# Four rows of the output stage loaded to one partition and repeated by TensorE instead of by the load

## The chip, the cores and the metric

The kernel runs on one core of one Trainium2 chip. The metric is the device time of one launch in microseconds (us): 4990.76 us, the median of three runs (4978.09 to 4993.18). The profiled execution took 4990.87 us, of which its trace spans 4988.1 us.

## The reference

One layer of a diffusion backbone runs over 128 context tokens and 512 latent tokens, of width 2048, in fp32: adaLN modulation, attention in two branches, an output projection with a gated residual, and then a PEER layer, in which each token picks 16 experts for each of 8 heads out of 16384 and gathers their rows. What the change touches is this part:

```python
    mod = jax.nn.silu(cond) @ p['w_ada'] + p['b_ada']
    sh1, sc1, g1, sh2, sc2, g2 = [m[:, None, :] for m in jnp.split(mod, 6, axis=-1)]
    ...
    x = x + g1 * (merged @ p['w_out'])

    h2 = rms_norm(x, p['norm2_g']) * (1 + sc2) + sh2
    x = x + g2 * peer_layer(h2, p['peer_w_query'], p['peer_sub_keys'], p['peer_u'], p['peer_v'])
```

The four rows of the title are g1, the gain norm2_g, the scale sc2 and the shift sh2. Each has 2048 numbers, one for each column and the same for all tokens of a group. With the tokens on the 128 partitions, an elementwise operation needs such a row in every partition.

## The kernel before

The 640 tokens are five blocks of 128, in three groups: group 0 is the context block, group 1 the first latent block, group 2 the other three latent blocks (`GROUP`, n = 1, 1, 3). For each group the kernel runs the branch products, the output stage, a norm, and the queries of the PEER layer. The three output stages lie at about 570 to 648 us, 1894 to 1959 us and 2564 to 2762 us of the span.

The output stage of a group has four chunks (`DCH` = 4) of 512 columns of `w_out`. The weights of a chunk come as two halves of 2 MB each, into a ring of three buffers (`WS` = 3), which SyncE fills in the order of use: a half is loaded as soon as TensorE has released the buffer of three halves before (`w_free`, L418). TensorE's `chunk` (L858) waits for a half, multiplies it with each of the n blocks (8 products of 128x128 by 128x512 for a half and a block, 16 for a chunk; the trace shows two matmul records for each such fp32 product), and releases it. In group 0 a panel of `w_ada` (2 MB, `ada`, L428 and L905) stands in the ring behind each chunk, so that group has three loads and three pieces of TensorE work to a chunk.

Around these loads SyncE issues, in its own order, the other transfers of the stage. Each of the four rows is read with `to_broadcast([P, D])`: 8 KB in DRAM, written 128 times, 1 MB into SBUF. Row g1 goes to `zone` when the transposes ahead of the stage are done (L623). In groups 0 and 1 the other three are issued after the second chunk's result was stored (`norm2_rows`, L617 to L619), ahead of the next halves. In group 2 sc2 and sh2 go out at L605 and L606, then g1 and the gain, all four ahead of the halves of the second chunk.

ScalarE copies each block's sums from PSUM to `zt` (`evac`, L1245), VectorE multiplies them by g1 and adds the residual (L1898 and L1900; in group 2 L1909 to L1913), and SyncE stores the result. Then VectorE forms (1 + sc2) * gain (L1547; in group 2 L1919), takes the norm, scales and shifts (L1557, L1558; in group 2 L1932, L1933), and TensorE turns the result for the queries (L886).

In group 2 the whole stage runs beside the PEER steps of group 1. For each token row GpSimd gathers 1 MB of expert rows (L766) into a ring of four buffers; VectorE takes a dot product with each (L1681, 16 of them), or adds each with a weight (L1691, 16), and only then frees the buffer. VectorE also chooses the experts of the next step in between (L1606 to L1660). Near its end this choice needs an exponential of ScalarE (`top_exps`, L1262): VectorE waits for `tk_exp` ahead of L1658. In ScalarE's order, the exponential of the first of these steps stands ahead of the evacuation of the stage's first block (`v in (0, 7)`).

PSUM has eight banks. The chunks use banks 0 to 1 or 0 to 3, the transposes banks 4 to 7, which are free while the output stage runs.

Of the kernel before, what the change touches and what calls it, by code (L numbers as in the profile page):

```python
# [8 lines left out]
D = 2048  # L9
# [67 lines left out]
U_OUT = tuple(u + 4 * DCH * g for u, g in zip(U_BR, GROUP))  # L77
U_QRY = tuple(u + DCH * g for u, g in zip(U_OUT, GROUP))

T_O = (NB, NB + 3, NB + 6)  # L80
T_M = tuple(t + g for t, g in zip(T_O, GROUP))
T_H = tuple(t + g for t, g in zip(T_M, GROUP))
EPS = 1e-6
SCALE = HD ** -0.5
LAM_INIT = 0.8 - 0.6 * math.exp(-0.3 * 0)
# [45 lines left out]
def build(nc, I, O):  # L131
# [34 lines left out]
    with ctx:  # L166
        def sb(name, shape, dt=f32):
            return ctx.enter_context(nc.sbuf_tensor(name, shape, dt))
# [8 lines left out]
        misc = sb("misc", [P, D])  # L177
        ident = sb("ident", [P, P])
        fold = sb("fold", [P, P])
        qts = sb("qts", [P, CH])  # L180
        small = sb("small", [P, 96])
        iota16 = sb("iota16", [P, TOPK])
# [14 lines left out]
        def zn(lo, n):  # L197
            return zone[:, lo:lo + n]
# [65 lines left out]
        def stay(c, lb):  # L264

            if c == DCH - 1:
                return zn(lb * CH, CH)
            places = [ac(A1 + 3 * D + CH * j, CH) for j in range(4)] + [zn(3 * CH, CH), zn(7 * CH, CH), zt[:, 3], zt[:, 4], qts[:, :]]
            return places[c * LAST + lb]

        def u_slot(i):

# [139 lines left out]
        def _(sp):  # L412
# [140 lines left out]
            for g in range(3):  # L553
# [46 lines left out]
                if g == 2:  # L600
                    sp.wait_ge(mm_done, U_OUT[2])
                    for lb in range(n):
                        sp.dma_start(xb[lb], xs[block_of(g, lb)]).then_inc(G["xt"][lb], 16)
                    sp.wait_ge(t_done, 4 * (T_M[g] + n))
                    sp.dma_start(A, mod[cnd:cnd + 1, 4 * D:5 * D].to_broadcast([P, D])).then_inc(s["row"], 16)  # L605
                    sp.dma_start(Bv, mod[cnd:cnd + 1, 3 * D:4 * D].to_broadcast([P, D])).then_inc(s["row"], 16)  # L606
                if g == 1:
                    sp.wait_ge(mm_done, U_OUT[1])
                    sp.dma_start(ac(A1, D), final_row).then_inc(fa_in, 16)
# [4 lines left out]

                def norm2_rows():

                    sp.dma_start(gain, I["norm2_g"].to_broadcast([P, D])).then_inc(s["row"], 16)  # L617
                    sp.dma_start(A, mod[cnd:cnd + 1, 4 * D:5 * D].to_broadcast([P, D])).then_inc(s["row"], 16)
                    sp.dma_start(Bv, mod[cnd:cnd + 1, 3 * D:4 * D].to_broadcast([P, D])).then_inc(s["row"], 16)  # L619

                if g == 0:
                    ada_rows(6)
                sp.dma_start(zn(0, D), mod[cnd:cnd + 1, 2 * D:3 * D].to_broadcast([P, D])).then_inc(G["g1"], 16)  # L623
                if g < 2:
                    sp.dma_start(zn(D, D), xs[0] if g else xp[0]).then_inc(G["xt"][0], 16)
                else:
                    sp.dma_start(gain, I["norm2_g"].to_broadcast([P, D])).then_inc(s["row"], 16)
                for c in range(DCH):
                    if g == 0:
                        ada(A_OUT + c)  # L630
# [91 lines left out]
        def _(pool):  # L722
# [9 lines left out]
            for n, v in enumerate(("lambda_q1", "lambda_k1", "lambda_q2", "lambda_k2")):  # L732
# [5 lines left out]
            nc.gpsimd.iota(iota16[:, :], pattern=[[1, TOPK]], base=0, channel_multiplier=0,  # L738
                           allow_small_or_imprecise_dtypes=True).then_inc(mats, 1)

            nc.gpsimd.memset(fold[:, :], 0.0).then_inc(mats, 1)
            for d in range(-3, 4):
                pool.wait_ge(mats, d + 7)
# [103 lines left out]
        def _(pe):  # L847
# [10 lines left out]
            def chunk(acts, n, i, step, blocks, u, bank_of, depth):  # L858

                for h in range(2):  # L860
                    wait_half(n + h, i, step)
                    for b in range(blocks):
                        if h == 0:
                            pe.wait_ge(bank_free, u + b + 1 + NB - depth)
                        ins = products(acts[:, h * (KT // 2):(h + 1) * (KT // 2)], b, n + h, bank_of(b), h == 0, h == 1)
                        if h == 1:
                            ins.then_inc(mm_done, 1)
                    if h == 0:
                        ins.then_inc(w_free, 1)
                release(u + blocks)  # L870

            def release(u):

# [174 lines left out]
            for g in range(3):  # L1048
# [55 lines left out]
                for lb in range(n if g == 2 else 0):  # L1104
                    for q in range(4):
                        pe.wait_ge(G["br"], B * DCH + q * n + lb + 1)
                        quarter(T_M[g] + lb, q, stay(q, lb))
                pe.wait_ge(t_free, (T_M[g] + n) * 4 + 4)
                for c in range(DCH):
                    chunk(mT[g], H_OUT[g] + 2 * c if g else RING_AT["out", 2 * c], 0, 0, n, U_OUT[g] + c * n, lambda b: bk(c * n + b), DEPTH[g])  # L1110
                    if g == 0:
                        ada(A_OUT + c)

# [127 lines left out]
        def _(sa):  # L1241
# [133 lines left out]
            for g in range(3):  # L1375
# [124 lines left out]
        def _(dve):  # L1500
# [39 lines left out]
            def norm(s, g, b, T0):  # L1540
# [2 lines left out]
                R, x = s["again"], xb[b % 2]  # L1543
                assert g != 2
                if b == 0 or (b == 1 and g == 3):
                    dve.wait_ge(s["row"], 48 * (1 + R) if b == 0 else 80)
# [326 lines left out]
            for g in range(3):  # L1873
# [28 lines left out]
                def residual_2(v):  # L1902

                    c, lb = v // n, v % n
                    x1 = nbuf[2][0][lb][:, c * CH:(c + 1) * CH]
                    if v == 0:
                        dve.wait_ge(G["g1"], 16 * (1 + B))
                    dve.wait_ge(bank_free, U_OUT[2] + v + NB + 1)
                    link(V.tensor_tensor(zt[:, v % 4], zt[:, v % 4], zn(c * CH, CH), ALU.mult))  # L1909
                    if c == 0:  # L1910
                        dve.wait_ge(G["xt"][lb], 16)
                    link(V.tensor_tensor(x1, x1, zt[:, v % 4], ALU.add))
                    signal(V.tensor_tensor_reduce(out=zt[:, v % 4], in0=x1, in1=x1, scale=1.0, scalar=0.0, op0=ALU.mult, op1=ALU.add,  # L1913
                                                  accum_out=small[:, 40 + 4 * lb + c:41 + 4 * lb + c]), G["ou"], B * DCH + v + 1)

                def scale_row():

                    dve.wait_ge(nrm[2]["row"], 48)
                    link(V.scalar_tensor_tensor(nbuf[2][2], nbuf[2][2], 1.0, nbuf[2][4], ALU.add, ALU.mult))  # L1919

                def norm_2(lb):
# [23 lines left out]
                        peer_step(1, PH + c, c % 2, PH + c)  # L1945
                        merge(c)
                if g < 2:
                    dve.wait_ge(G["g1"], 16 * (1 + B))
# [163 lines left out]
```

## Time and profile before

| | us |
|---|---|
| median of three runs | 4990.76 |
| lowest, highest | 4978.09, 4993.18 |
| the profiled execution | 4990.87 |
| its span in the trace | 4988.1 |
| PE busy | 3316.5 (66%) |
| DVE busy | 2717.3 (54%) |
| POOL busy | 1853.9 (37%) |
| ACT busy | 452.8 (9%) |

The page gives the whole span first: how busy each engine is, and in 40 slices of 125 us each engine, TensorE's granted clock (in tenths) and the DMA engines. The three output stages lie in slices 5 to 6, 16 and 21 to 23 of the 40:

```profile
PE   4869989899698898999999861333333333333334
DVE  2330128988134202577778888656565656565653
PEclk7989999999799999999999985555555555555555
DMA  9978988899899678999999999999999999999998
```

A digit of 9 means 90% and more. In these slices both TensorE and the DMA engines are near full, so neither line alone tells which one a stage waits for. For that one has to go to the stage itself: to TensorE's own instructions in order of time, with what ended each idle time before them.

### The profile page before, as it was taken

The numbers are of one execution on the slowest core, as the hardware profiler recorded it, in microseconds if no ns is written. First come the engines' busy times: TensorE is split into PE (matmuls) and PEld (weight loads), VectorE is DVE, ScalarE is ACT, GpSimd is POOL, SyncE is SP. The second block draws the span as 40 slices with busy tenths as digits, with TensorE's granted clock in tenths as the row PEclk, the third lists the DMA queues.
The fourth block names the chain that finished last, engine by engine and source line by source line (L and its number), as shares of the span: only waits on it lengthen the run. The fifth ranks groups of instructions, "written<-read, shape, count | busy, mean of one in ns | idle before, by whom it ended". The sixth has DMA issues, their size and how long they took to land.

```text
span 4988.1 us, 32667 instructions
## 1 busy us (share of the span) xinstructions
PE 3316.5 (66%) x11402; PEld 1292.2 (26%) x11402; DVE 2717.3 (54%) x4132; ACT 452.8 (9%) x824; POOL 1853.9 (37%) x1365
## 2 busy tenths in 40 slices
PE   4869989899698898999999861333333333333334
PEld 0333333344244443444444430000000000000000
DVE  2330128988134202577778888656565656565653
ACT  0010010000122201111110110000000000000000
POOL 0000004444233000244434565564545555555542
PEclk7989999999799999999999985555555555555555
DMA  9978988899899678999999999999999999999998
GB/s 380 385 292 326 357 303 313 324 357 368 348 391 404 250 283 301 357 365 366 370 389 396 379 410 373 421 421 421 421 411 418 421 421 421 415 416 421 421 421 336
DMA packets 407517, 1869.35 MB, mean 375 GB/s; under 512 B 30016, under 2 KB 33632, under 8 KB 238160
## 3 DMA queue, kind: packets, MB, share of 16 engines
q0 software_dynamic: 187200, 1347.98, 66.1%
q1 hardware_dynamic: 220176, 519.60, 28.0%
q8 instruction: 75, 1.23, 0.1%
q14 instruction: 66, 0.54, 0.0%
HBM read 1835.65 MB, written 33.13 MB: 375 GB/s over the span
## 4 chain that ended last, share of the span: by engine, by line
DMA 47%; PE 33%; DVE 11%; issue 5%; POOL 2%; ACT 1%; SPq 0%; DVEq 0%; POOLq 0%; ACTq 0%; PEldq 0%
PE ps L854 24%; DMA activations<-in_peer_v,zt 19%; DMA big<-in_peer_v,zt 15%; DMA big<-in_w_in 3%; DMA big<-in_peer_u,sel 3%; DVE big L1744 2%; DMA big<-in_peer_v,zone 2%; PE ps L1232 2%; DMA big<-in_peer_w_query 2%; DMA big<-in_w_ada 2%; PE ps L954 2%; PE ps L1014 2%; DVE big L1691 1%; PE ps L992 1%; PE ps L905 1%
## 5 line engine op out<-in xcount | busy, mean ns | idle before, releaser
L854 PE MATMUL ps<-big,activations 128*128 128x512 f32 x4096 | 1806.6, 601 | 89.6 <-ACT zt L1245 27.4
L854 PEld LDWEIGHTS ps<-big,activations 128*128 128x128 f32 x4096 | 782.0, 193 | 1097.5 <-issue 1006.4
L2066 DVE CUSTOM_DVE_ANT_0 big<-big,activations 128x2048 f32<-128x2048 f32 x256 | 585.2, 2291 | 492.2 <-DMA big<-in_peer_u,sel 492.1
L836 POOL DMA_INDIRECT big<-in_peer_u,sel x384 | 505.8, 1317 | 594.8 <-DVE zt L2066 501.6
L1232 PE MATMUL ps<-activations,zt 128*32 128x512 f32 x1536 | 333.8, 959 | 506.8 <-DMA activations<-in_peer_v,zt 506.8
L1232 PE MATMUL ps<-big,zt 128*32 128x512 f32 x1536 | 350.8, 1033 | 471.7 <-DMA big<-in_peer_v,zt 369.3
L2066 DVE CUSTOM_DVE_ANT_0 big<-big,zone 128x2048 f32<-128x2048 f32 x128 | 291.4, 2291 | 212.3 <-DMA big<-in_peer_u,sel 212.1
L842 POOL DMA_INDIRECT big<-in_peer_v,zt x192 | 306.2, 1595 | 155.8 <-PE ps L1232 126.2
L805 POOL DMA_INDIRECT big<-in_peer_u,sel x128 | 213.2, 1666 | 292.9 <-DVE zone L1744 258.4
L1744 DVE CUSTOM_DVE_ANT_0 big<-big 128x2048 f32<-128x2048 f32 x128 | 289.1, 2290 | 42.3 <-DMA big<-in_peer_u,sel 41.0
L1691 DVE SCALAR_TENSOR_TENSOR big<-big,work 128x2048 f32<-128x2048 f32 x115 | 270.5, 2352 | 62.2 <-DMA big<-in_peer_v,sel 58.7
L1681 DVE CUSTOM_DVE_ANT_0 big<-big 128x2048 f32<-128x2048 f32 x114 | 259.8, 2289 | 68.7 <-DMA big<-in_peer_u,sel 67.7
L842 POOL DMA_INDIRECT activations<-in_peer_v,zt x192 | 216.2, 1126 | 177.9 <-PE ps L1232 128.8
L749 POOL DMA_DIRECT2D mod_rows<-work x12 | 6.2, 520 | 662.9 <-DVE work L1535 662.9
L854 PE MATMUL ps<-big 128*128 128x512 f32 x544 | 242.3, 604 | 11.9 <-DMA big<-in_w_in 10.3
L766 POOL DMA_INDIRECT big<-in_peer_v,sel x96 | 169.6, 1767 | 196.2 <-DVE big L1691 148.4
L1232 PEld LDWEIGHTS ps<-activations,zt 128*32 128x32 f32 x1536 | 40.0, 136 | 780.3 <-DMA activations<-in_peer_v,zt 738.6
L1232 PEld LDWEIGHTS ps<-big,zt 128*32 128x32 f32 x1536 | 47.1, 148 | 735.7 <-DMA big<-in_peer_v,zt 553.4
L766 POOL DMA_INDIRECT big<-in_peer_u,sel x96 | 153.4, 1598 | 224.0 <-DVE work L1681 181.6
L1195 PE MATMUL ps<-small,zt 128*128 128x16 f32 x48 | 14.3, 378 | 329.4 <-DVE zt L1865 329.4
L811 POOL DMA_INDIRECT big<-in_peer_v,zone x128 | 122.0, 953 | 270.1 <-PE ps L954 211.2
L1785 DVE TENSOR_REDUCE small<-ps 128x1 f32<-128x640 f32 (+1 forms) x80 | 57.4, 718 | 259.7 <-PE ps L992 259.0
(215 smaller groups left out, 2734.4 us busy)
## 6 DMA issues: line engine op xcount, KB each, us to landing
big<-in_w_in SPq DMA_DIRECT2D x84, 2048.0 KB, 10.2
big<-in_w_ada SPq DMA_DIRECT2D x48, 2048.0 KB, 12.4
big<-in_w_out SPq DMA_DIRECT2D x24, 2048.0 KB, 14.6
big<-in_peer_w_query SPq DMA_DIRECT2D x24, 2048.0 KB, 9.6
big<-in_w_branch_a SPq DMA_DIRECT2D x12, 2048.0 KB, 12.6
big<-in_w_branch_b SPq DMA_DIRECT2D x12, 2048.0 KB, 9.7
big<-z_blocks SPq DMA_DIRECT2D x20, 512.0 KB, 13.1
big<-in_peer_u,sel POOLq DMA_INDIRECT x626, 10.6
```

Of the source, the lines that this page charges most:

```text
L766: pool.indirect_dma_start(slot(j), None, eu if j < TOPK else ev, bass.IndirectOffsetOnAxis(ap=sel[:, q, j % TOPK:j % TOPK + 1], axis=0)).t ...
L805: pool.indirect_dma_start(slot(m), None, eu, bass.IndirectOffsetOnAxis(ap=sel[:, t % 2, k:k + 1], axis=0)).then_inc(ring_in[m % RING], 16)
L811: pool.indirect_dma_start(v_slot_0(n), None, ev, bass.IndirectOffsetOnAxis(ap=idx_t0[:, n:n + 1], axis=0)).then_inc(v_in[n % VR_0], 16)
L836: pool.indirect_dma_start(u_slot(m), None, eu, bass.IndirectOffsetOnAxis(ap=sel[:, t % 2, k:k + 1], axis=0)).then_inc(u_in[m % UR], 16)
L842: pool.indirect_dma_start(v_slot(m), None, ev, bass.IndirectOffsetOnAxis(ap=idx_v[(t - 1) % 3][:, k:k + 1], axis=0)).then_inc(v_in[m % VR] ...
L854: ins = nc.tensor.matmul(bank(bk), acts[:, k, b * P:(b + 1) * P], w[:, n % WS, k], start=(start and k == 0), stop=(stop and k == KT // 2 - 1))
L954: ins = nc.tensor.matmul(ps[32 * j:32 * j + 32, 7 * 512:8 * 512], spread_0[q % 2][:, i * 32:(i + 1) * 32], v_slot_0(n)[:, j * CH:(j + 1) * ...
L1232: ins = nc.tensor.matmul(ps[32 * j:32 * j + 32, q * 512:(q + 1) * 512], spread[(t - 1) % 2][:, k * 32:(k + 1) * 32], v_slot(m)[:, j * CH:( ...
L1681: V.tensor_tensor_reduce(out=t, in0=t, in1=hcur, scale=1.0, scalar=0.0, op0=ALU.mult, op1=ALU.add, accum_out=dots[:, k:k + 1]).then_inc(ri ...
L1691: signal(V.scalar_tensor_tensor(acc, tile(TOPK + k), coef[:, k:k + 1], acc, ALU.mult, ALU.add), ring_free, m * 32 + RING + TOPK + k + 1)
L1744: V.tensor_tensor_reduce(out=slot(m), in0=slot(m), in1=hcur, scale=1.0, scalar=0.0, op0=ALU.mult, op1=ALU.add, accum_out=dots_0[:, m:m + 1 ...
L2066: V.tensor_tensor_reduce(out=x, in0=x, in1=h_of[ph], scale=1.0, scalar=0.0, op0=ALU.mult, op1=ALU.add, accum_out=dots_s[t % 2][:, k:k + 1] ...
```

## The change

The rows are loaded as they are, 8 KB to one partition. A tile `ones` (1 x 128) is filled once by GpSimd. For each row TensorE forms four products, `ones` (1 x 128) by 512 numbers of the row (1 x 512), into banks 4 to 7, and ScalarE copies the four banks over the row's tile, all 128 partitions. The products stand between and within the chunks (`ROW_AT` gives chunk and half for each row), the copies ahead of certain evacuations (`ROW_OUT`). VectorE waits for the copies in place of the loads. The counters of the transposes (`T_O`, `T_M`, `T_H`) are moved by the four rows.

```diff
-T_O = (NB, NB + 3, NB + 6)
+ROWS = 4
+T_O = (NB, NB + 3 + ROWS, NB + 6 + 2 * ROWS)
 T_M = tuple(t + g for t, g in zip(T_O, GROUP))
-T_H = tuple(t + g for t, g in zip(T_M, GROUP))
+T_R = tuple(t + g for t, g in zip(T_M, GROUP))
+T_H = tuple(t + ROWS for t in T_R)
...
+        def row_of(g, i):
+
+            return (zn(0, D), nbuf[g][2], nbuf[g][3], nbuf[g][4])[i]
+
+        ROW_AT = ({(0, 1): 0, (2, 0): 1, (2, 1): 2, (3, 0): 3},) * 2 + ({(0, 0): 0, (1, 0): 1, (1, 1): 2, (2, 0): 3},)
+        ROW_OUT = ({1: (0,), 2: (1,), 3: (2, 3)},) * 2 + ({0: (0,), 3: (1,), 6: (2, 3)},)
...
                 def norm2_rows():
 
-                    sp.dma_start(gain, I["norm2_g"].to_broadcast([P, D])).then_inc(s["row"], 16)
-                    sp.dma_start(A, mod[cnd:cnd + 1, 4 * D:5 * D].to_broadcast([P, D])).then_inc(s["row"], 16)
-                    sp.dma_start(Bv, mod[cnd:cnd + 1, 3 * D:4 * D].to_broadcast([P, D])).then_inc(s["row"], 16)
+                    sp.dma_start(gain[0:1], I["norm2_g"]).then_inc(s["row"], 16)
+                    sp.dma_start(A[0:1], mod[cnd:cnd + 1, 4 * D:5 * D]).then_inc(s["row"], 16)
+                    sp.dma_start(Bv[0:1], mod[cnd:cnd + 1, 3 * D:4 * D]).then_inc(s["row"], 16)
 
                 if g == 0:
                     ada_rows(6)
-                sp.dma_start(zn(0, D), mod[cnd:cnd + 1, 2 * D:3 * D].to_broadcast([P, D])).then_inc(G["g1"], 16)
+                sp.dma_start(zn(0, D)[0:1], mod[cnd:cnd + 1, 2 * D:3 * D]).then_inc(G["g1"], 16)
...
+            nc.gpsimd.memset(ones[:, :], 1.0)
...
                     if h == 0:
                         ins.then_inc(w_free, 1)
+                        behind(0)
                 release(u + blocks)
+                behind(1)
...
+                def row_turn(c, h):
+
+                    if (c, h) not in ROW_AT[g]:
+                        return
+                    i = ROW_AT[g][c, h]
+                    if i == 0:
+                        pe.wait_ge(G["g1"], 16 * (1 + B))
+                    if i == 1:
+                        pe.wait_ge(nrm[g]["row"], 48 * (1 + R))
+                    for q in range(4):
+                        pe.wait_ge(t_free, (T_R[g] + i) * 4 + q + 1)
+                        nc.tensor.matmul(bank(4 + q), ones[:, :], row_of(g, i)[0:1, q * CH:(q + 1) * CH],
+                                         start=True, stop=True).then_inc(t_done, 1)
...
+                def row_out(i):
+
+                    for q in range(4):
+                        sa.wait_ge(t_done, (T_R[g] + i) * 4 + q + 1)
+                        nc.scalar.activation(row_of(g, i)[:, q * CH:(q + 1) * CH], bank(4 + q), ACT.Copy).then_inc(t_free, 1)
+
                 for c in range(DCH):
                     for lb in range(n):
                         v = c * n + lb
+                        for i in ROW_OUT[g].get(v, ()):
+                            row_out(i)
                         if v == 0:
                             sa.wait_ge(G["zt"], 2 * DCH * (n + R) + ZTS[g])
```

The loads of group 2 (L605, L606, L623, L627) are changed in the same way. In VectorE's program the waits for the loads ahead of L1547, L1898, L1909 and L1919 become waits for `t_free`.

## Rows read from the trace of the kernel before

**Rows 1.** The page: the shares of the chain that ended last, by engine.
```profile
DMA 47%; PE 33%; DVE 11%; issue 5%; POOL 2%; ACT 1%; SPq 0%; DVEq 0%; POOLq 0%; ACTq 0%; PEldq 0%
```

**Rows 2.** Timeline of PE, output stage of group 0: start, duration, instruction, idle before.
```profile
569.82 14.00 PE L854 MATMUL ps<-big,activations 128*128 128x512 f32 x32 [1.06 <-ACT activations L1251]
583.97 1.90 PE L905 MATMUL ps<-big,small 128*2 128x512 f32 x16
588.48 15.70 PE L854 MATMUL ps<-big,activations 128*128 128x512 f32 x32 [2.61 <-DMA big<-in_w_out]
...
606.15 14.00 PE L854 MATMUL ps<-big,activations 128*128 128x512 f32 x32
625.52 3.59 PE L905 MATMUL ps<-big,small 128*2 128x512 f32 x16 [5.37 <-DMA big<-in_w_ada]
630.94 16.93 PE L854 MATMUL ps<-big,activations 128*128 128x512 f32 x32 [1.83 <-DMA big<-in_w_out]
```

**Rows 3.** Windows, group 0: stretch, engines' busy us, then clock, DMA share, GB/s.
```profile
588.00:604.00 16.00, 15.53 (x32) 6.61 (x32) 0.00 (x0) 0.00 (x0) 0.00 (x0) 0.89 0.94 356
...
613.00:631.00 18.00, 10.81 (x34) 3.32 (x32) 3.12 (x4) 0.60 (x1) 0.00 (x0) 0.78 1.02 404
```

**Rows 4.** Timeline of SyncE's queue in the same stage.
```profile
606.87 0.39 SPq L617 DMA_DIRECT2D big<-in_norm_g  x1
...
608.25 0.43 SPq L428 DMA_DIRECT2D big<-in_w_ada  x1
```

**Rows 5.** The 12 DMAs of bias rows (tile in_b_ada), 8 KB each: time to landing.
```profile
DMA to landing us min/median/max: 1.8/4.9/5.8
```

**Rows 6.** DMA issues between 613 and 625 us: count, size, us to landing.
```profile
x_blocks<-zt SPq DMA_DIRECT2D x1, 256.0 KB, 15.9
```

**Rows 7.** Timeline of PE, output stage of group 1.
```profile
1894.01 14.00 PE L854 MATMUL ps<-big,activations 128*128 128x512 f32 x32 [1.06 <-ACT activations L1251]
...
1922.75 13.97 PE L854 MATMUL ps<-big,activations 128*128 128x512 f32 x32 [0.46 <-PE ps L854]
1943.30 16.11 PE L854 MATMUL ps<-big,activations 128*128 128x512 f32 x32 [6.58 <-DMA big<-in_w_out]
```

**Rows 8.** Timeline of SyncE's queue in the same stage.
```profile
1925.56 0.45 SPq L617 DMA_DIRECT2D big<-in_norm_g  x1
...
1928.17 5.72 SPq L419 DMA_DIRECT2D big<-in_w_out  x2
```

**Rows 9.** Timeline of ACT, output stage of group 2.
```profile
2575.89 1.28 ACT L1262 ACT_TABLE_LOAD   x1 [12.36 <-DVE work L1630]
2577.18 0.31 ACT L1262 ACTIVATE work<-work 128x16 f32<-128x16 f32 x1
...
2591.36 0.60 ACT L1245 ACTIVATE zt<-ps 128x512 f32<-128x512 f32 x1 [13.77 <-PE ps L854]
```

**Rows 10.** Timeline of DVE in the same stage.
```profile
2583.51 0.16 DVE L1658 RECIPROCAL work<-work 128x1 f32<-128x1 f32 x1
...
2594.35 2.29 DVE L1681 CUSTOM_DVE_ANT_0 big<-big 128x2048 f32<-128x2048 f32 x1 [0.94 <-DMA big<-in_peer_u,sel]
...
2762.30 0.69 DVE L1909 TENSOR_TENSOR zt<-zt,zone 128x512 f32<-128x512 f32 x1
```

**Rows 11.** Waits of DVE between 2556 and 2614 us: total, times, longest.
```profile
DVE big L1681 <- DMA big<-in_peer_u,sel: 9.0, 9, 1.7
```

**Rows 12.** Timeline of PE, first and last chunk of group 2 (three blocks each).
```profile
2563.59 41.47 PE L854 MATMUL ps<-big,activations 128*128 128x512 f32 x96 [1.24 <-ACT activations L1251]
...
2696.91 41.47 PE L854 MATMUL ps<-big,activations 128*128 128x512 f32 x96 [3.45 <-DMA big<-in_w_out]
```

**Rows 13.** DMA queues between 2587 and 2600 us: packets, MB, share of 16 engines.
```profile
q0 software_dynamic: 576, 4.19, 77.9%
q1 hardware_dynamic: 576, 1.18, 24.2%
```

**Rows 14.** The gathers issued between 720 and 800 us: time to landing.
```profile
DMA to landing us min/median/max: 7.1/9.3/12.9
```

More of the change, by code:

```diff
@@ L179, in build @@
         fold = sb("fold", [P, P])
+        ones = sb("ones", [1, P])
         qts = sb("qts", [P, CH])
@@ L615, in norm2_rows @@
                 def norm2_rows():
-                    sp.dma_start(gain, I["norm2_g"].to_broadcast([P, D])).then_inc(s["row"], 16)
-                    sp.dma_start(A, mod[cnd:cnd + 1, 4 * D:5 * D].to_broadcast([P, D])).then_inc(s["row"], 16)
-                    sp.dma_start(Bv, mod[cnd:cnd + 1, 3 * D:4 * D].to_broadcast([P, D])).then_inc(s["row"], 16)
+                    sp.dma_start(gain[0:1], I["norm2_g"]).then_inc(s["row"], 16)
+                    sp.dma_start(A[0:1], mod[cnd:cnd + 1, 4 * D:5 * D]).then_inc(s["row"], 16)
+                    sp.dma_start(Bv[0:1], mod[cnd:cnd + 1, 3 * D:4 * D]).then_inc(s["row"], 16)
                 if g == 0:
                     ada_rows(6)
-                sp.dma_start(zn(0, D), mod[cnd:cnd + 1, 2 * D:3 * D].to_broadcast([P, D])).then_inc(G["g1"], 16)
+                sp.dma_start(zn(0, D)[0:1], mod[cnd:cnd + 1, 2 * D:3 * D]).then_inc(G["g1"], 16)
                 if g < 2:
@@ L626, in _ @@
                 else:
-                    sp.dma_start(gain, I["norm2_g"].to_broadcast([P, D])).then_inc(s["row"], 16)
+                    sp.dma_start(gain[0:1], I["norm2_g"]).then_inc(s["row"], 16)
                 for c in range(DCH):
@@ L856, in products, with chunk @@
                 return ins
-            def chunk(acts, n, i, step, blocks, u, bank_of, depth):
+            def chunk(acts, n, i, step, blocks, u, bank_of, depth, behind=lambda h: None):
                 for h in range(2):
@@ L1108, in _ @@
                 pe.wait_ge(t_free, (T_M[g] + n) * 4 + 4)
+                def row_turn(c, h):
[10 more added lines that the diff above has]
+                                         start=True, stop=True).then_inc(t_done, 1)
                 for c in range(DCH):
-                    chunk(mT[g], H_OUT[g] + 2 * c if g else RING_AT["out", 2 * c], 0, 0, n, U_OUT[g] + c * n, lambda b: bk(c * n + b), DEPTH[g])
+                    chunk(mT[g], H_OUT[g] + 2 * c if g else RING_AT["out", 2 * c], 0, 0, n, U_OUT[g] + c * n, lambda b: bk(c * n + b), DEPTH[g], lambda h: row_turn(c, h))
                     if g == 0:
@@ L1545, in norm @@
                 if b == 0 or (b == 1 and g == 3):
-                    dve.wait_ge(s["row"], 48 * (1 + R) if b == 0 else 80)
+                    if g == 3:
+                        dve.wait_ge(s["row"], 48 if b == 0 else 80)
+                    else:
+                        dve.wait_ge(t_free, (T_R[g] + ROWS) * 4 + 4)
                     link(V.scalar_tensor_tensor(A, A, 1.0, gain, ALU.add, ALU.mult))
@@ L1906, in residual_2 @@
                     if v == 0:
-                        dve.wait_ge(G["g1"], 16 * (1 + B))
+                        dve.wait_ge(t_free, (T_R[2] + 1) * 4 + 4)
                     dve.wait_ge(bank_free, U_OUT[2] + v + NB + 1)
@@ L1916, in scale_row @@
                 def scale_row():
-                    dve.wait_ge(nrm[2]["row"], 48)
+                    dve.wait_ge(t_free, (T_R[2] + ROWS) * 4 + 4)
                     link(V.scalar_tensor_tensor(nbuf[2][2], nbuf[2][2], 1.0, nbuf[2][4], ALU.add, ALU.mult))
@@ L1947, in _ @@
                 if g < 2:
-                    dve.wait_ge(G["g1"], 16 * (1 + B))
+                    dve.wait_ge(t_free, (T_R[g] + 1) * 4 + 4)
                     for v in range(DCH * n):
```

## The prediction

> **What bounds the kernel now.** I read four views, in this order. First the page's chain that ended last: it is 47% DMA and 33% PE [rows 1], so both a transfer taken away and TensorE work added can move the end; which of them does, only the stage tells. Second, TensorE's timeline of each output stage, for its idle times and what ended them. In group 0 TensorE waits 2.61 us for a half of w_out, 5.37 us for a panel of w_ada and 1.83 us for the next half [rows 2]. Third, the windows around two of these waits: granted clock 0.89 and 0.78, DMA share 0.94 and 1.02 [rows 3]. So part of each stretch ran at the lower of the two levels, 1.2 instead of 2.4 GHz, and the durations agree: the same 32 records took 14.00 us in two chunks, 15.70 and 16.93 us in the two behind a wait, the same 16 of w_ada 1.90 and 3.59 us [rows 2]. This stage is bound by its loads and pays for it in idle time and in clock. In group 1 one wait is left, 6.58 us ahead of the last chunk, which then took 16.11 us [rows 7]; the rest of that stage is TensorE at full clock. Fourth, VectorE's waits in group 2, where the gathers set the pace: 9.0 us in nine waits between 2556 and 2614 [rows 11].
>
> **The loads removed.** Twelve rows of 1 MB become 8 KB each. At the 404 GB/s of the stretch at 613 [rows 3] one is 1.05 MB / 404 = 2.6 us of all DMA engines. Three are issued at 606.87, ahead of the w_ada panel at 608.25 [rows 4], which comes 5.37 us late; their 7.8 us cover this wait and the 1.83 behind it. The fourth, g1, lies ahead of the half that is 2.61 us late, and is worth as much. I let all three waits go.
>
> **The products added.** This is the term that decides. A chunk is 16 products (two halves of 8) and shows as 32 records in 14.00 us [rows 2], so a product of 512 columns is 14.00 / 16 = 0.88 us, not 0.44. A row of the change is four products: 3.5 us, four rows 14.0 us. The trace has no product over a single partition, so I bound it by its neighbours. High end: the chunk at a mixed clock, 16.93 / 16 = 1.06 us, 17 us for four rows. Low end: the panel of w_ada, 8 products of 512 columns in 1.90 us, 0.24 us each [rows 2], 3.8 us for four rows; but these have two output rows each and write four parts of a bank, while the new ones have 128 outputs, as those of a chunk. I take 0.88.
>
> One page bears on the low end. The Trainium skill, TensorE: Matmul & The Clock Gate, section Why this matters for your kernels, says that a single product over 32 rows takes as long as one over 128. By it a row costs 3.5 us, as taken; no row of this trace shows a product over so few rows.
>
> **Group 0.** Now the stage runs from 569.82 to 630.94 + 16.93 = 647.87, 78.05 us [rows 2]. Afterwards: four chunks 4 x 14.00 = 56.0, three panels 3 x 1.90 = 5.7, the rows 14.0, and 0.3 between chunks, 0.9: 76.6. Gain 1.4 us. What is late next? A half is issued when its buffer comes free and needed two pieces of work later, at the least a half and a panel, 8.9 us, and mostly a row more; with fewer bytes ahead of it that suffices. The new wait is TensorE's for the three small loads ahead of row 1. Behind it on TensorE queue the second half of the third chunk and all that follows. By this sum chunk 1 ends at about 603.7, its store goes out at about 606, the loads are issued by 607.7, and row 1 stands at 612.9. Loads of 8 KB landed in 1.8 to 5.8 us, median 4.9 [rows 5]: no wait. With the high price of a product the group loses 1.6; with the loads late it loses more (below). ScalarE's copies, 16 of 0.60 us [rows 9] in a group, cost nothing in groups 0 and 1: ScalarE waits for the chunks there. The last ones lie in the last half-chunk, 7 us, so VectorE's chain behind the stage finds its rows ready. If that cover were gone, 2.4 us a row.
>
> **Group 1.** Now 1894.01 to 1943.30 + 16.11 = 1959.41, 65.4 us [rows 7]. Afterwards 56.0 + 14.0 + 0.9 = 70.9: a loss of 5.5 us, though the wait of 6.58 us and the low clock behind it (16.11 - 14.00 = 2.1) are gone; 8.7 us of gain pay for 14.0 us of products. The loads ahead of the last half, from 1925.56 to 1928.17 [rows 8], are those that made it late. Row 1 comes due at about 1933.1, and the small loads are issued by about 1930, behind 1 MB of output (2.6 us): landing at the median would make TensorE wait 1.4 us more. Loss 6.9, between 4.3 (no wait, and a gap or two less) and 10.
>
> **Group 2.** TensorE has room here: its last block is done at 2696.91 + 41.47 = 2738.4 [rows 12] and taken by VectorE at 2762.30 [rows 10], so 14 us of rows hide in 23.9. Two other things count. First a gain: of VectorE's waits, 9.0 us [rows 11] come from gathers that share the DMA engines with the loads. With the queues both full, each gets as many packets, 576 and 576, but 4.19 MB for the gathers against 1.18 MB [rows 13], since a gather's packets are longer; so 4 MB less ahead of the weights' two halves empties that queue early, and the gathers have the engines to themselves. They would then land in some 7.1 to 9.3 us [rows 14] after issue, and with four buffers and a dot product of 2.29 us [rows 10] part of each wait stays. Second a cost, hidden in ScalarE's order: row 0's copies stand ahead of the exponential. The row's products come after the first half of the chunk, 2563.59 + 41.47 / 2 = 2584.3 [rows 12], end at 2587.8, the last copy at 2588.5; then the table load and the exponential, 1.28 + 0.31 and some 0.2 [rows 9]: 2590.3. VectorE needs it at 2583.51 [rows 10]. Behind this wait are queued all its dot products, so it stands 6.8 us. The four buffers fill meanwhile: the next four dots run without the 0.94 us [rows 10] of before them, and the others wait less. Following them one by one with a landing of 8 us, the sixteenth ends at about 2616.9, against 2616.7: gain and stall cancel. I take 0; the ends are -6.8 (nothing returned) and +9 (all waits gone and the stall hidden).
>
> **The sum** against the profiled execution, 4990.87 us, which is 0.1 from the median: +1.4 - 6.9 + 0 = -5.5, so 4996.4. All behind the stages follows by dependence, and I let the shifts pass to the end.
>
> **Rivals.**
> 1. Products over one partition are short (0.24 us). Group 0: 56 + 5.7 + 3.8 + 0.9 = 66.4, of which the loads, that need their 8 us each, may let 9 us be gained; group 1 gains 65.4 - 60.7 = 4.7, less 1; group 2 perhaps 2. 4976. Against it: the number of outputs is that of a full product.
> 2. Group 2 pays: the freed queue gives back the 9.0 us and the stall hides. 4988. For it, DMA is full there; against it, VectorE's stall is plain in ScalarE's order.
> 3. The stall of group 2 stays whole and products cost the high price: 4996.4 + 6.8 + 2 x 3 = 5009. It decides where gathers land later than about 9 us after issue.
> 4. The small loads are late. A store of 256 KB issued in this stage took 15.9 us to land [rows 6], since the queue ahead of it was full. At 15.9 row 1 of group 0 would come at 623.5 instead of 612.9, that of group 1 at 1946 instead of 1933: 10.6 and 11.4 more, 5018. From about 6 us of landing group 0 starts to lose, group 1 from about 3.
> 5. The change doesn't do what it says: the weights' waits come from the ring of three buffers and not from the rows. Then the rows' 14 us add to 78 in group 0, part of them inside the waits. With 8 us lost there: 5006.
>
> One page speaks against the change where rival 4 does. The Trainium skill, DMA: Bandwidth & Descriptors, section Bandwidth, says that transfers under 64 KB are dominated by their descriptors, and wants 1 MB at least. By it the small loads waste the engines; the bias rows, 4.9 us [rows 5], show only their latency.
>
> **How the numbers follow.** The forecast has 0.56, rival 1 0.10, rival 2 0.12, rival 3 0.10, rival 4 0.06, rival 5 0.06. The range leaves out the outer part of rivals 1, 4 and 5: 4983 to 5010. About 0.3%, 15 us, is what a measurement here can tell from no change; so faster (below 4975.9) has only part of rival 1 and a tail, 0.09; slower (above 5005.7) has rivals 3, 4 and part of 5, 0.18; the same 0.73.
>
> **What would show it.** Right: in group 0 no wait of TensorE for w_ada; each row's four products last 3.5 us; group 1's stage 70 to 73 us; VectorE idle for 6 to 7 us ahead of the L1658 that now stands at 2583.51, released by ScalarE. Wrong: rows of products under 2 us or over 5; a wait of TensorE of over 3 us ahead of row 1; halves still late in group 0; VectorE's end of group 2's stage moved by over 5 us.

## The result: slower by 0.64%, outside the range

| | us |
|---|---|
| kernel before, median of 5 runs | 4990.76 (4978.09 to 4994.51) |
| changed kernel, median of 5 runs | 5020.47 (5013.49 to 5030.88) |
| ratio, 95% interval | 1.0064 (1.0050 to 1.0077) |
| forecast, range | 4996.4 (4983 to 5010) |
| profiled execution of the changed kernel | 5030.88, its span 5029.2 |

The profiled execution is the slowest of the five, so the traces lie 41.1 us apart (5029.2 - 4988.1) where the medians lie 29.7 apart. A second profiled execution of the same kernel is among the experiments. The page of the changed kernel, its busy times and the chain:

```profile
PE 3379.6 (67%) x11498; PEld 1315.2 (26%) x11498; DVE 2716.2 (54%) x4132; ACT 481.8 (10%) x872; POOL 1864.2 (37%) x1366
...
DMA 44%; PE 37%; DVE 11%; issue 4%; POOL 2%; ACT 1%; SPq 0%; another core or an unknown queue 0%; DVEq 0%; POOLq 0%; ACTq 0%; PEldq 0%
```

Four points of the chain went over to TensorE, 37% for 33%, and DMA has 44% for 47% [rows 1]. TensorE is busy 63.1 us longer. The products, at 3.67 us a row (below), make 12 x 3.67 = 44 of that; what the other 19 are, only the stages tell. TensorE's timeline of group 1's output stage (start, duration, instruction, idle before):

```profile
1907.42 14.00 PE L865 MATMUL ps<-big,activations 128*128 128x512 f32 x32 [1.06 <-ACT activations L1278]
1921.72 5.16 PE L1133 MATMUL ps<-zone,ones 1*128 1x512 f32 x8 [0.30 <-PE ps L865]
1926.81 15.85 PE L865 MATMUL ps<-big,activations 128*128 128x512 f32 x32
1942.97 7.10 PE L865 MATMUL ps<-big,activations 128*128 128x512 f32 x16 [0.30 <-PE ps L865]
1951.31 4.10 PE L1133 MATMUL ps<-activations,ones 1*128 1x512 f32 x8 [1.23 <-DMA activations<-mod_rows]
1955.34 10.08 PE L865 MATMUL ps<-big,activations 128*128 128x512 f32 x16
1965.57 4.64 PE L1133 MATMUL ps<-activations,ones 1*128 1x512 f32 x8
1970.14 9.51 PE L865 MATMUL ps<-big,activations 128*128 128x512 f32 x16
...
1984.56 9.13 PE L865 MATMUL ps<-big,activations 128*128 128x512 f32 x16
```

The wait for w_out of 6.58 us [rows 7] is gone, and the longest wait left is 1.23 us, for the small loads. Yet the stage takes 86.3 us, from 1907.42 to 1993.69, where it took 65.4. No work is missing its data; the same work is slower. A half-chunk behind a row takes 9.13 to 10.08 us where half of a 14.00 us chunk is due, and the rows take 4.10 to 5.16. The windows over both stages (busy us of PE, PEld, DVE, ACT, POOL, then granted clock, DMA share, GB/s) say why:

```profile
570.00:656.10 86.10, 84.54 (x208) 32.58 (x208) 9.02 (x10) 11.36 (x20) 0.52 (x1) 0.90 0.81 291
1907.40:1993.70 86.30, 84.28 (x160) 33.75 (x160) 13.70 (x13) 12.81 (x21) 0.00 (x0) 0.84 0.66 234
```

TensorE is busy for 84.28 of 86.30 us, and its granted clock is 0.84: part of a stage with hardly any idle time ran at 1.2 instead of 2.4 GHz. The kernel before had 0.95 in this stage. In group 0 it was 0.89 before, with TensorE idle for 10.2 of 78.1 us; now it is 0.90 with 1.6 of 86.1 idle, so there the idle time went and the low clock stayed. Behind rows 0 and 1:

```profile
590.27 15.12 PE L865 MATMUL ps<-big,activations 128*128 128x512 f32 x32
607.36 7.13 PE L865 MATMUL ps<-big,activations 128*128 128x512 f32 x16
615.06 3.69 PE L1133 MATMUL ps<-activations,ones 1*128 1x512 f32 x8 [0.57 <-DMA activations<-mod_rows]
618.69 8.83 PE L865 MATMUL ps<-big,activations 128*128 128x512 f32 x16
```

Where the clock is full, a row is 3.67 us and a half 7.13. Along the span the 41.1 us come in as +0.2 ahead of group 0's stage, +8.0 in it (78.05 to 86.0), +5.2 between the two stages, +20.9 in group 1's, -0.1 up to group 2, +8.0 in group 2, and -1.0 in the rest. The 5.2 us lie in code that is unchanged: that stretch took 1246.1 us in the profiled execution of the kernel before, and 1247.2 to 1256.7 in the eleven of this and the later kernels, 1252.9 in the one that has neither products nor small loads. Scatter of single executions, with the one of before at its low end, would explain it; with one profile of the kernel before it is not shown.

### The profile page after: what moved, and what is told of

Read it like the earlier page. It is cut to its first block, busy times and chain, and to the rows that moved or that the text cites. A ratio compares the mean times of both kernels' runs of the same rounds, so it can differ in the third digit from the quotient of the medians.

```text
span 5029.2 us, 32914 instructions
## 1 busy us (share of the span) xinstructions
PE 3379.6 (67%) x11498; PEld 1315.2 (26%) x11498; DVE 2716.2 (54%) x4132; ACT 481.8 (10%) x872; POOL 1864.2 (37%) x1366
## 3 DMA queue, kind: packets, MB, share of 16 engines
q0 software_dynamic: 187200, 1347.98, 65.7%
## 4 chain that ended last, share of the span: by engine, by line
DMA 44%; PE 37%; DVE 11%; issue 4%; POOL 2%; ACT 1%; SPq 0%; another core or an unknown queue 0%; DVEq 0%; POOLq 0%; ACTq 0%; PEldq 0%
PE ps L865 27%; DMA activations<-in_peer_v,zt 17%; DMA big<-in_peer_v,zt 16%; DMA big<-in_w_in 3%; DVE big L1782 2%; PE ps L1259 2%; DMA big<-in_w_ada 2%; PE ps L967 2%; PE ps L1027 2%; DMA big<-in_peer_u,sel 2%; DMA big<-in_peer_v,zone 2%; PE ps L1005 1%; DVE big L1729 1%; PE ps L918 1%; DMA big<-in_peer_w_query 1%
## 5 line engine op out<-in xcount | busy, mean ns | idle before, releaser
L847 POOL DMA_INDIRECT big<-in_peer_u,sel x384 | 509.4, 1327 | 593.1 <-DVE zt L2104 499.6
L816 POOL DMA_INDIRECT big<-in_peer_u,sel x128 | 216.2, 1689 | 286.3 <-DVE zone L1782 250.9
L777 POOL DMA_INDIRECT big<-in_peer_u,sel x96 | 159.3, 1660 | 221.3 <-DVE work L1719 176.7
```

Of the source, the lines that this page charges most:

```text
L777: pool.indirect_dma_start(slot(j), None, eu if j < TOPK else ev, bass.IndirectOffsetOnAxis(ap=sel[:, q, j % TOPK:j % TOPK + 1], axis=0)).t ...
L816: pool.indirect_dma_start(slot(m), None, eu, bass.IndirectOffsetOnAxis(ap=sel[:, t % 2, k:k + 1], axis=0)).then_inc(ring_in[m % RING], 16)
L847: pool.indirect_dma_start(u_slot(m), None, eu, bass.IndirectOffsetOnAxis(ap=sel[:, t % 2, k:k + 1], axis=0)).then_inc(u_in[m % UR], 16)
```

## The experiments

Theory: products over a single partition, though they follow each other without idle time, leave TensorE's granted clock to fall, and all work of the stage pays for that. The rivals: TensorE is slow because it waits (for small loads or weights); the loads were never what the stage waited for; the cost lies in group 2's order of ScalarE. Stages are told by length, from the start of the first chunk to the end of the last.

### The same products over all 128 partitions

```diff
-        ones = sb("ones", [1, P])
+        ones = sb("ones", [P, P])
...
-            nc.gpsimd.memset(ones[:, :], 1.0)
+            nc.gpsimd.memset(ones[:, :], 0.0).then_inc(ones_ok, 1)
+            pool.wait_ge(ones_ok, 1)
+            nc.gpsimd.memset(ones[0:1, :], 1.0).then_inc(ones_ok, 1)
...
-                        nc.tensor.matmul(bank(4 + q), ones[:, :], row_of(g, i)[0:1, q * CH:(q + 1) * CH],
+                        nc.tensor.matmul(bank(4 + q), ones[:, :], row_of(g, i)[:, q * CH:(q + 1) * CH],
```

> The changed kernel with one edit: the stationary operand of the row products is 128x128 (first row ones, the rest zeros) and the moving one takes all 128 partitions of the row's tile, so each product is a full one with the same outputs. Theory (the granted clock falls because a product over one partition leaves TensorE nearly idle): granted clock 1.00 in the stages of groups 0 and 1, the pieces behind a row again 7.1 and 14.0 us, stage of group 0 at 77 to 79 us instead of 86.1, of group 1 at 71 to 73 instead of 86.3, and the whole 15 to 25 us below the changed kernel's 5020 (ratio to before 1.001 to 1.004). Rival (the clock falls because of the short gaps or waits around the rows, or from TensorE's total load): both stages stay at 85 to 87 us and the ratio at 1.006.

Measured: 5000.87 us, median of 12, against 4990.76; ratio 1.0019 (1.0011 to 1.0028). Timeline of PE in group 1, and the windows over groups 0 and 1:

```profile
1895.38 14.00 PE L868 MATMUL ps<-big,activations 128*128 128x512 f32 x32 [1.06 <-ACT activations L1281]
1909.68 3.67 PE L1136 MATMUL ps<-zone,ones 128*128 128x512 f32 x8 [0.30 <-PE ps L868]
1913.19 13.90 PE L868 MATMUL ps<-big,activations 128*128 128x512 f32 x32
...
1935.73 3.70 PE L1136 MATMUL ps<-activations,ones 128*128 128x512 f32 x8 [1.20 <-DMA activations<-mod_rows]
1939.26 7.03 PE L868 MATMUL ps<-big,activations 128*128 128x512 f32 x16
```
```profile
567.70:645.00 77.30, 75.90 (x208) 30.76 (x208) 9.03 (x10) 11.35 (x20) 0.52 (x1) 1.00 0.90 326
1895.40:1967.30 71.90, 69.89 (x160) 29.96 (x160) 13.71 (x13) 12.77 (x21) 0.00 (x0) 1.00 0.78 280
```

Same number of products, same order, same loads, and a wait of 1.20 us for them at the same place; only the rows that take part differ. The clock is 1.00, the halves behind a row take 7.03 us, and the stages 77.3 and 71.9 us instead of 86.0 and 86.3. That is the theory, and it accounts for 8.7 + 14.4 = 23.1 us of the profiled executions; the medians lie 19.6 apart (5020.47 - 5000.87). The result of a product is the same in both, since 127 of its rows meet a zero. The edit widens both operands of the product, so which of the two the clock answers to is not told apart.

### The products added to the kernel before, its loads kept

```diff
+                    for q in range(4):
+                        nc.tensor.matmul(bank(4 + q), ident[0:1, :], misc[0:1, q * CH:(q + 1) * CH], start=True, stop=True)
```

They stand at the change's places, and nobody reads them. A second kernel takes `ident[:, :]` and `misc[:, ...]`, all 128 partitions.

> The kernel before, all its loads as they are, with 4 x 4 products over one partition added in each stage at the places of the change; nothing reads them, nothing waits for them. Theory: the clock falls in group 1's stage: 65.4 + 14.7 + some 9 of clock, less the wait of 6.6 for the late half that is covered: 80 to 84 us; group 0's stage 84 to 90. Rival (the copies, the waits for them or the small loads lower the clock): group 1's stage 72 to 75 us at clock 1.00. Ratio to before by the theory 1.003 to 1.006, by the rival 1.001 to 1.003.

> The same as e2_before_plus_one_row but with the products over all 128 partitions. Theory: 3.5 to 3.7 us a row and the clock of the stages at 1.00 except behind waits for loads: group 1's stage 72 to 74 us, some 8 to 10 less than with one partition. Rival: the same as with one partition, within 2 us.

Measured: 5010.34 us (ratio 1.0033, 1.0020 to 1.0046) over one partition, 5001.12 (1.0012, 1.0003 to 1.0021) over all. Group 1, two lines of the one, then two of the other, then the window of each:

```profile
1927.04 3.70 PE L1118 MATMUL ps<-misc,ident 1*128 1x512 f32 x8
1930.66 15.62 PE L854 MATMUL ps<-big,activations 128*128 128x512 f32 x32
```
```profile
1915.82 3.67 PE L1118 MATMUL ps<-misc,ident 128*128 128x512 f32 x8
1919.33 13.90 PE L854 MATMUL ps<-big,activations 128*128 128x512 f32 x32
```
```profile
1912.90:1989.30 76.40, 75.80 (x160) 31.24 (x160) 13.70 (x13) 3.23 (x5) 0.00 (x0) 0.93 0.87 319
```
```profile
1901.70:1971.90 70.20, 69.60 (x160) 30.04 (x160) 13.71 (x13) 3.22 (x5) 0.00 (x0) 1.00 0.93 346
```

The pair repeats the difference without the change's loads, copies and waits: clock 0.93 against 1.00, stage 76.5 against 70.3. The sign is as expected, both sizes were missed: I had expected 80 to 84 and 72 to 74 us. With one-partition products the changed kernel loses 14.4 us here, this one 6.2. In group 0 the stage took 88.7 us at a clock of 0.87 with no wait of TensorE above 0.33 us, as expected (84 to 90), and 82.2 at 0.96 over all partitions, where a wait of 3.06 us for w_out stands. There the clock is lower than in the changed kernel (0.90). So how far the clock falls is not given by the products alone.

### The small loads alone

The changed kernel without the products and copies; the tiles' other 127 rows stay as they were. What is left out is in the expectation.

> The changed kernel with only its small loads: no products of the rows and no copies, so 127 partitions keep old numbers in the four rows' tiles (the rows are missing there; the output and the experts that are chosen follow from that, the amount of work does not). It gives the gain of the loads alone. My sum: group 0's three waits go, stage 62 to 64 us instead of 78.05; group 1's wait goes, stage 57 to 58 instead of 65.4; VectorE's waits in group 2 between its first dot products fall from 9.0 to under 6 us. Whole: ratio 0.993 to 0.996. Rival (the waits for weights come from the ring of three buffers): group 0 at 72 us or more.

Measured: 4967.51 us, ratio 0.9947 (0.9934 to 0.9960), stages 64.3 and 56.8 us. Group 1 is the bare work, 4 x 14.00 and the gaps, and all its waits are gone. So the weights' waits did come from the 1 MB loads, and taking them away is worth 8.6 us in group 1 and 13.8 in group 0. The stages had been expected at 62 to 64 and 57 to 58, so both sizes were nearly met. In group 2 the expectation for the gathers, waits under 6 us, fails. VectorE's waits for them, over the same 58 us of the stage as rows 11:

```profile
DVE big L1717 <- DMA big<-in_peer_u,sel: 8.6, 7, 2.3
```

8.6 us where the kernel before has 9.0. Over this stretch the kernels without a stall and with small loads (this one and three below) have 6.9 to 8.6 us, those with the 1 MB loads 8.7 to 10.3. Four megabytes less ahead of the weights give the gathers little.

### The exponential ahead of row 0's copies

The kernel with the products over 128 partitions, and in group 2:

```diff
+                        if g == 2 and v == 0:
+                            top_exps(PH + 5)
                         for i in ROW_OUT[g].get(v, ()):
                             row_out(i)
```

(the second call stays ahead of the evacuation of v == 7)

> e1_full_rows with ScalarE's first exponential of group 2's stage put ahead of row 0's copies. Theory A of the prediction (the stall of 6.9 us and the gathers' gain cancel): the stall goes, and from the first product of the stage to the first product behind it (L1225's first, 396.1 us in e1_full_rows) 2 to 5 us are gained; ratio 0.0005 to 0.001 lower than e1_full_rows. Theory B (the gathers have nothing to give, the stall costs in full): 7 us gained. Theory C (the DMA engines set the pace there): no gain.

Measured: 4999.92 us, ratio 1.0021 (1.0012 to 1.0030), so in the whole nothing that can be told from 1.0019. I had expected 0.0005 to 0.001 less. VectorE's waits in group 2 over the 58 us of rows 11, of the changed kernel, of the one with full rows, and of this one (engine, line, releaser: total, times, longest):

```profile
DVE work L1696 <- ACT work L1289: 7.1, 1, 7.1
...
DVE big L1719 <- DMA big<-in_peer_u,sel: 3.1, 4, 1.6
```
```profile
DVE work L1699 <- ACT work L1292: 6.9, 1, 6.9
...
DVE big L1722 <- DMA big<-in_peer_u,sel: 2.8, 5, 1.1
```
```profile
DVE big L1724 <- DMA big<-in_peer_u,sel: 6.9, 7, 2.7
```

The stall of 6.9 us goes; the waits for gathers rise from 2.8 to 6.9, and the group is 3.2 us shorter (392.9 against 396.1, one execution each). Of the stall, 4.1 us had been paid back by buffers that filled during it.

### The kernel before with three loads later

```diff
-                    if g < 2 and c == 1:
+                    if g < 2 and c == 2:
```

in SyncE's program, at the condition that guards `norm2_rows()`: in groups 0 and 1 the three 1 MB loads go out behind the last weights of the stage. Not one byte is saved, and there are no products. In group 1 the same condition also guards a store of 1 MB of finished output. It moves along: before, it stood ahead of the last half of w_out, now behind it.

```profile
1924.91 0.59 SPq L648 DMA_DIRECT2D out<-activations  x1
```
```profile
1939.94 0.37 SPq L648 DMA_DIRECT2D out<-activations  x1
```

> The kernel before with one edit: in groups 0 and 1 SyncE issues its three 1 MB row loads behind the store of the third chunk instead of the second, so behind the halves of the last chunk. If these loads did harm only because they stood ahead of weights: group 0's stage 66 to 70 us instead of 78.05, group 1's 57 to 59 instead of 65.4, and nothing is given back by the norm behind the stage; ratio 0.995 to 0.997. Rival (the bytes count, wherever they stand): the norm waits for its rows or the queries' weights come late, and the ratio is 0.999 to 1.000.

Measured: 4975.74 us, ratio 0.9971 (0.9962 to 0.9980), stages 67.8 and 56.9 us, 0.1 from the bare work in group 1. What the loads and the store are worth apart in group 1 is not told by this run; in the kernel with the small loads alone the store stayed where it was and no wait was left. This is the best version of the study that computes everything. The wait for w_ada did not go away, it stands behind the stage:

```profile
627.92 14.00 PE L854 MATMUL ps<-big,activations 128*128 128x512 f32 x32 [1.82 <-DMA big<-in_w_out]
647.69 3.59 PE L905 MATMUL ps<-big,small 128*2 128x512 f32 x16 [5.77 <-DMA big<-in_w_ada]
```

There TensorE's panel is not what comes next for the norm, and the 5.77 us lie beside VectorE's work: from the end of the stage to the first product that waits for the norm it is 12.2 us, as before.

### The changed kernel once more

No edit.

> The changed kernel once more, unedited, beside the others of this call and with a second profile. Its stages should again be 8 and 15 to 21 us longer than before's, at a granted clock of 0.84 to 0.93 in group 1's; the 5.2 us that the first profile lost between the two stages, where nothing was changed, should not come back if they were the scatter of one execution, and should if the change did them. Ratio 1.005 to 1.0075.

Measured: 5030.67 us, median of 6, ratio 1.0078 (1.0062 to 1.0094), stages 85.4 and 84.6 us. The clock's fall is no accident of one execution; it was 0.92 and 0.86 in the two stages. Group 2 came out at +5.0 us instead of +8.0. The stretch between the first two stages, which was to lose its 5.2 us if they were scatter, came at 1254.4 us, 8.3 above the kernel before.

### Four products side by side

Here each small load writes partitions 0, 32, 64 and 96, and product q takes partition 32 q, to see whether the four of a row then run at once; the exponential stands first.

```diff
-                    sp.dma_start(gain[0:1], I["norm2_g"]).then_inc(s["row"], 16)
+                    sp.dma_start(gain[0:97:32], I["norm2_g"].to_broadcast([4, D])).then_inc(s["row"], 16)
...
-                        nc.tensor.matmul(bank(4 + q), ones[:, :], row_of(g, i)[0:1, q * CH:(q + 1) * CH],
+                        nc.tensor.matmul(bank(4 + q), ones[32 * q:32 * q + 1, :], row_of(g, i)[32 * q:32 * q + 1, q * CH:(q + 1) * CH],
```

> The changed kernel with each row loaded to the partitions 0, 32, 64 and 96 (32 KB), and its four products taken from one of these each, so that they can run side by side in the array; the exponential stands first as in e5_full_rows_exp_first. If they run side by side a row takes 0.9 to 1.0 us instead of 3.7 and the clock stays: group 0's stage 66 to 69 us, group 1's 61 to 63, ratio 0.996 to 0.998. If they run one after the other, as in the changed kernel: 3.7 us a row, falling clock, ratio 1.005. If side by side but the clock falls all the same: stages 3 to 8 us longer than the first figures.

Measured: 4988.31 us, median of 12, ratio 0.9999 (0.9989 to 1.0009), stages 72.7 and 67.8 us. The row's time is as expected, the stages (66 to 69 and 61 to 63) and the ratio (0.996 to 0.998) were missed. Group 1:

```profile
1910.78 1.14 PE L1133 MATMUL ps<-zone,ones 1*128 1x512 f32 x8 [0.30 <-PE ps L865]
1911.85 14.00 PE L865 MATMUL ps<-big,activations 128*128 128x512 f32 x32
...
1936.19 1.69 PE L1133 MATMUL ps<-activations,ones 1*128 1x512 f32 x8 [2.94 <-DMA activations<-mod_rows]
1937.82 9.93 PE L865 MATMUL ps<-big,activations 128*128 128x512 f32 x16
```

A row is 1.14 us instead of 3.67, still over single partitions, and the chunk behind it takes 14.00 us, the full clock; the halves behind rows 2 and 3 take 7.13 each. Only behind the wait of 2.94 us for the small loads does the clock fall, and in group 0 behind one of 1.78 us. So no row of 1.14 us is followed by slow work where no wait stood; but row 1 now comes due earlier, and the loads are late for it. The Trainium skill, TensorE: Matmul & The Clock Gate, section Part 3: Packing small matmuls — row/col tiling, gives 3.07 times for four products over 32 rows each, placed so. The trace, with one row each, agrees: 3.67 / 1.14 = 3.2.

### The small loads one chunk earlier

Two kernels with `if g < 2 and c == 0:` as the condition that guards `norm2_rows()`, one made from the changed kernel, one from that with four products side by side. In group 1 the 1 MB store of finished output moves ahead with the small loads here too.

> The changed kernel with the three small loads of groups 0 and 1 issued behind the store of the first chunk instead of the second, so that TensorE doesn't wait for them ahead of row 1. Theory (the clock falls by the one-partition products themselves): group 1's stage loses the 1.2 us of waiting and little more: 80 to 85 us at a clock of 0.84 to 0.92, ratio 1.005 to 1.007. Rival (in the changed kernel it is this wait that lets the clock fall, and so the 8 to 10 us between its group 1, 86.3, and that of e2_before_plus_one_row, 76.5): 75 to 77 us, ratio 1.003.

> e8_four_row_groups with the small loads issued a chunk earlier, in the same way. There the waits for them, 1.78 and 2.94 us, were each followed by a half of 10.0 instead of 7.1 us. If the wait is what let the clock fall there: group 0's stage 67 to 69 us instead of 72.7, group 1's 61 to 63 instead of 67.8, ratio 0.997 to 0.999. If the short rows do it: the halves behind row 1 stay at 9 to 10 us.

Measured: the first 5019.34 us, ratio 1.0058 (1.0045 to 1.0071), stages 83.7 and 80.0; the second 4983.01 us, ratio 0.9988 (0.9979 to 0.9997), stages 73.8 and 65.2. Group 1 of the first, with its window, then of the second:

```profile
1915.84 3.99 PE L1133 MATMUL ps<-zone,ones 1*128 1x512 f32 x8 [0.30 <-PE ps L865]
1919.76 17.03 PE L865 MATMUL ps<-big,activations 128*128 128x512 f32 x32
...
1944.12 5.01 PE L1133 MATMUL ps<-activations,ones 1*128 1x512 f32 x8
1949.06 9.16 PE L865 MATMUL ps<-big,activations 128*128 128x512 f32 x16
```
```profile
1901.50:1981.50 80.00, 79.20 (x160) 32.19 (x160) 13.70 (x13) 12.83 (x21) 0.00 (x0) 0.89 0.71 252
```
```profile
1925.69 8.83 PE L865 MATMUL ps<-big,activations 128*128 128x512 f32 x16 [2.38 <-DMA big<-in_w_out]
1934.45 1.14 PE L1133 MATMUL ps<-activations,ones 1*128 1x512 f32 x8
1935.52 7.13 PE L865 MATMUL ps<-big,activations 128*128 128x512 f32 x16
```

In the first, TensorE waits for nothing in this stage beyond the 0.30 us between chunks, and its clock falls all the same: a chunk of 17.03 us right behind a row. So the wait for the small loads is not the cause of the fall; at the most it adds to it. In the second the wait for the small loads is gone and one for w_out of 2.38 us has come ahead of it, 3.50 us in group 0, with a slow half behind; 65.2 and 73.8 us are not the 61 to 63 and 67 to 69 I had expected. This is faster than the kernel before by 0.12%, by an interval that ends at 0.9997, and not as fast as moving the three loads alone.

## Why the prediction was wrong

**The step that failed: the price of a product, and the 14.00 us of each chunk, assumed the full clock.** "I take 0.88" was right at full clock, 3.67 us a row where I had 3.5 (row 0 of group 0, and the rows over 128 partitions). What failed is the sum around it, which gave the chunks 14.00 us each because TensorE would be busy. I read the clock in rows 3 and rows 7 as something that falls behind a wait, and concluded that with the waits gone it stays. It falls beside these products too. In group 1 the chunks took 65.7 us instead of 56.0 and the rows 18.95 instead of 14.0. My high end, 1.06 us a product, had this in part for the rows (they came out at 1.18) and not at all for the chunks. The forecast's own sign of being wrong, a row of over 5 us, stands in group 1 twice, 5.16 and 5.05. With the clock kept full, in the run with full rows, the same kernel came out at 5000.87, 4.5 us over the forecast.

**Group 0**, forecast 76.6 us: 86.0, at full clock 77.3. The waits for w_ada and the last half went, as forecast; a wait of 0.57 us for small loads stood ahead of row 1. In the second execution (85.4 us) a half of w_out was still 1.29 us late.

**Group 1**, forecast 70.9 and 1.4 of wait, 72.3: 86.3, at full clock 71.9. The small loads made TensorE wait 1.23 us, as the sum had it. So the products at full clock and the wait were right, the clock was not.

**Group 2**, forecast 0. VectorE takes the last block of the stage, in the changed kernel:

```profile
2800.23 0.69 DVE L1947 TENSOR_TENSOR zt<-zt,zone 128x512 f32<-128x512 f32 x1
```

From the start of the stage it is 202.5 us to this step, 202.7 in the second execution, and 198.7 in the kernel before [rows 10, 12]: 3.8 and 3.9 us lost where the sum had 0. The stall came as forecast, 7.1 us for 6.8. The waits for gathers over the 58 us of rows 11 fell from 9.0 to 3.1, so that stall and waits together are 10.2 us for 9.0: in this stretch they nearly cancel, by the buffers filled in the meantime, as forecast. The other 2.6 of the 3.8 us come later in the stage and were not followed up. That less load traffic would help the gathers was right only in small part (6.9 to 8.6 us where no stall stands, against 8.7 to 10.3 with the 1 MB loads). By the ends of the stage the stall costs some 4 us: the four executions that have it end 1.3 to 3.9 us later than before, the four with small loads and without it 0.9 to 1.8 us earlier. What is left of the +8.0 and +5.0 lies behind the stage, in code that is unchanged, and that stretch takes 196.0 to 203.8 us over all twelve profiled executions, 199.0 in the kernel before; single executions tell no more there.

**The rivals.** The first (short products) is refuted as written, 3.67 us a row; its price becomes true only with the four side by side, and then the time was 4988, not 4976. The second asked that the 9.0 us of waits for gathers go and the stall hide; neither did in full. The third had the stall whole; some 4 of its 7 us stayed. The fourth asked for small loads of 15.9 us; they made TensorE wait 0.57 and 1.23. The fifth, that the waits come from the ring, is refuted by the small loads alone: none is left in group 1, and two of 1.13 and 0.84 us in group 0. None had the clock. One would have been due: the trace of before showed two levels of the clock in these very stages, and the change put a kind of product between the chunks that no row of it shows, which bounds its cost in time but not what it does to its neighbours. By the panel of w_ada, 1.90 us at one level and 3.59 at the other [rows 2], the low one nearly doubles the work behind each of 12 rows, so the range had to reach well beyond 5010.

**The sum**: forecast +5.5 us, profiled +41.1. Of the 35.6 between them 9.4 lie in group 0, 14.0 in group 1, 8.0 in group 2 (3.8 of them in its stage), 5.2 in the unchanged code between the stages, and -1.0 in the rest.

**What stays open**: how far the clock falls beside the same one-partition products. In group 1 it was 0.84 and 0.86 in the changed kernel (86.3 and 84.6 us), 0.89 with its loads early (80.0) and 0.93 in the kernel before with the products added (76.5). In group 0 the order is another one: 0.90 and 0.92, 0.92, and 0.87. So a cause that makes the changed kernel's clock the lower one, the wait of 1.2 us ahead of row 1, the copies or the small loads, would fit group 1 and not group 0. Part of it may be chance: in two executions of the changed kernel the last half of group 1 took 9.13 and 7.13 us. Which of these counts wasn't tried.

## What to carry to other kernels

Moving three loads behind the last weights (one character, which in group 1 moves a 1 MB store as well) gained about 14 us of 4990, with no new work; the change, which took the bytes of the row loads away and paid with products, lost 30, and 41 the second time. When a load makes the weights late, first ask whether it can be issued later. And when TensorE gets small products in a stage that it bounds, count what they do to the granted clock of the work around them, not their own duration alone: over one partition they cost the chunks of group 1 another 9.7 us. If they are needed, put four side by side at partitions 0, 32, 64 and 96 (1.14 us for four), or feed them all 128 partitions.

## What the runs showed of the hardware

TensorE's granted clock can fall with the engine busy almost without a break. Over group 1 it was 0.84 with products over one partition and 1.00 with products over 128 that take as long at full clock, 3.67 us a row; PE was busy for 98% and 97% of the two stretches. In the trace of the kernel before I had only seen it fall behind waits. Second, four fp32 products of 512 columns over the partitions 0, 32, 64 and 96 took 1.14 us together against 3.67 one behind the other, and left the clock of the work behind them full where no wait stood ahead.
